# Values of attention A and of the windowed attention, forget gates and shared rotary key made as one block of 680 columns, tokens on partitions, at the start of each layer

## What is computed

```python
h = rms_norm(x, g_mix_pre[i])
z = h @ w_in[i]                                    # 1024 -> 3112 columns
aq, ak, av, af, bcq, bckv, bkpe, cq, ck, cv = jnp.split(z, offsets, axis=-1)
log_f = jax.nn.log_sigmoid(af + b_forget[i])       # 8 forget gates
log_f_cum = jnp.cumsum(log_f, axis=1)
ya = blocked_attention(aq, ak, av, 64 ** -0.5, True, log_f_cum)   # 8 heads of 64
# B: latent attention from bcq, bckv; its rotary key is bkpe (32 columns), shared by the heads
# C: attention over a window of 128, 8 query heads, 2 key/value heads of 64: cq, ck, cv (128 columns)
gates = jax.nn.sigmoid(h @ w_gate[i] + b_gate[i])
merged = ga * (ya @ w_branch_a[i]) + gb * (yb @ w_branch_b[i]) + gc * (yc @ w_branch_c[i])
x = x + rms_norm(merged @ w_out[i], g_mix_post[i])
```

## Time and profile before

| | |
|---|---|
| median of 3 runs | 1970.95 us (1969.31 to 1971.2) |
| the profiled execution | 1971.17 us, span 1969.4 us |
| PE (matmul) busy | 1934.1 us, 98% |
| DVE, ACT, POOL busy | 55%, 42%, 5% |
| DMA | 176.17 MB, 89 GB/s over the span |
| PE's waits on other engines, the longest | `xt` of the residual 8.4, first DMA 4.0, `kB` 2.7, `kC` 2.3 us |

### The profile page before, as it was taken

How to read it: one execution, slowest core, us unless ns; L and a number is a source line. 1 busy time by engine, 2 the same in 40 slices (tenths; PEclk the granted TensorE clock), 3 DMA queues, 4 the chain that set the end, 5 groups by cost and what they waited for, 6 DMA issues and landing times. The chain is left out here.

```text
span 1969.4 us, 25861 instructions
## 1 busy us (share of the span) xinstructions
PE 1934.1 (98%) x9269; PEld 1593.0 (81%) x9269; DVE 1081.1 (55%) x1896; ACT 834.0 (42%) x1417; POOL 107.1 (5%) x85
## 2 busy tenths in 40 slices
PE   8999999999999999999999999999999999999997
PEld 6888887888878888888868888878888788888886
DVE  5444446445477777425674444555445777773266
ACT  4254436543344444314433544455433544442243
POOL 0000000101101111000000000001110011110000
PEclk9999999999999999999999999999999999999999
DMA  5411242213513333332343112421144133333322
GB/s 156 113 40 47 65 97 75 65 43 125 175 32 102 99 95 99 103 111 97 84 124 96 33 54 65 97 76 59 51 150 137 52 98 96 96 97 118 98 84 75
DMA packets 256979, 176.17 MB, mean 89 GB/s; under 512 B 52180, under 2 KB 240880, under 8 KB 256624
## 3 DMA queue, kind: packets, MB, share of 16 engines
q1 hardware_dynamic: 256744, 174.70, 30.2%
q10 hardware_dynamic: 136, 0.16, 0.1%
HBM read 170.44 MB, written 4.36 MB: 89 GB/s over the span
## 5 line engine op out<-in xcount | busy, mean ns | idle before, releaser
L602 PE MATMUL psum<-xnh,wh 128*128 128x512 f32 (+1 forms) x1424 | 573.0, 402 | 7.3 <-DVE kC L1576 2.3
L1307 DVE TENSOR_TENSOR wl<-raw,wh 128x1024 fp32r<-128x1024 f32 (+1 forms) x276 | 363.6, 1317 | 368.9 <-ACT wh L1002 368.2
L602 PE MATMUL psum<-xnh,wl 128*128 128x512 f32 (+1 forms) x1424 | 556.9, 391 | 0.0
L602 PE MATMUL psum<-xnl,wh 128*128 128x512 f32 (+1 forms) x1424 | 556.2, 391 | 0.0
L1002 ACT ACTIVATE wh<-raw 128x1024 fp32r<-128x1024 f32 (+1 forms) x276 | 290.3, 1052 | 422.3 <-PE psum L602 413.1
L602 PEld LDWEIGHTS psum<-xnh,wh 128*128 128x128 f32 (+1 forms) x1424 | 267.3, 188 | 64.9 <-issue 14.9
L602 PEld LDWEIGHTS psum<-xnh,wl 128*128 128x128 f32 (+1 forms) x1424 | 266.6, 187 | 58.9 <-issue 0.5
L602 PEld LDWEIGHTS psum<-xnl,wh 128*128 128x128 f32 (+1 forms) x1424 | 267.3, 188 | 49.9 <-issue 0.2
L1057 ACT ACTIVATE PT<-psum 128x256 f32<-128x256 f32 (+3 forms) x192 | 78.5, 409 | 176.0 <-PE psum L773 175.3
L1450 DVE CUSTOM_DVE_ANT_0 Sp<-psum,ptok 128x128 f32<-128x128 f32 (+3 forms) x128 | 62.5, 489 | 116.2 <-issue 59.5
L602 PE MATMUL psum<-wh,fh 128*128 128x512 f32 x288 | 112.0, 389 | 0.0
(11 more groups left out here) (248 smaller groups left out, 2873.4 us busy)
## 6 DMA issues: line engine op xcount, KB each, us to landing
raw<-in_w_up_dram SPq DMA_DIRECT2D x88, 512.0 KB, 3.7
raw<-in_w_gate_dram SPq DMA_DIRECT2D x48, 512.0 KB, 3.7
raw<-in_w_down_dram SPq DMA_DIRECT2D x44, 512.0 KB, 3.5
raw<-in_w_in_dram SPq DMA_DIRECT2D x40, 512.0 KB, 3.8
raw<-in_w_out_dram SPq DMA_DIRECT2D x16, 512.0 KB, 3.6
raw<-in_w_ple_gate_dram SPq DMA_DIRECT2D x16, 512.0 KB, 3.6
raw<-in_w_in_dram SPq DMA_DIRECT2D x16, 256.0 KB, 3.3
raw<-in_w_branch_a_dram SPq DMA_DIRECT2D x8, 512.0 KB, 3.3
```

What stands on the lines that cost most here:

```text
L602: ins = pe.matmul(out, left, right, start=start and n == 0, stop=stop and n == 2)
L1307: dve.tensor_tensor(low[:, 0:n], raw[(L * NCH + c) % RAW][:, 0:n], hi[:, 0:n].bitcast(F32), ALU.subtract).then_inc(w_lo.sem, 1)
```

## The change

The 512 columns of `vA`, 8 gates, 32 of the shared key and 128 of `vC` are one block of 680 columns, made first in the layer, in eight chunks `first` (one for each 128 input channels, 680 floats wide, three DMAs). Tokens come out on partitions: each chunk is used for 4 blocks of tokens x 2 halves of 340 columns x 3 matmuls, and the eight banks hold all sums. The matmuls of chunks 0 and 1 are done block by block of tokens, since the banks come free in pairs as the norm goes on. ACT evicts the first 340 columns of each block to `vA`, DVE the other 340 in four pieces to `vA`, `kft` (gates and key) and `vC`. `kft` is turned by four transposes beside the first key chunk and copied to `kf`, from where the gates go on as before. The halves of chunks 2 and 3 lie in extra places (`front_x`). `vC` is no longer turned. The stage of attention A begins after the last `qA` chunk and has `qC` x 4, `kC` and the first gate chunk; that of attention C has 11 chunks. The first score steps of attention A wait for the `qA` banks one by one.

```diff
-    [("kf", 0)] + [("kA", m) for m in range(4)] + [("qA", m) for m in range(4)] + [("vA", m) for m in range(4)]
-    + [("qC", m) for m in range(4)] + [("vC", 0), ("kC", 0)]
+    [("first", m) for m in range(KT)] + [("kA", m) for m in range(4)] + [("qA", m) for m in range(4)]
+    + [("qC", m) for m in range(4)] + [("kC", 0)]
...
+ST_KA = KT
+ST_A = ST_KA + 8
...
+EXTRA.update({2: 0, 3: 1})
...
+FW = 340
+WIDTH = {"first": 2 * FW}
+F_GATE, F_PE, F_VC = 512, 520, 552
...
+        if kind == "first":
+            return [(full[:, 0:F_PE], w_in[L, :, m, CA_V:CA_V + 520]),
+                    (full[:, F_PE:F_VC], w_in[L, :, m, CB_PE:CB_PE + 32]),
+                    (full[:, F_VC:2 * FW], w_in[L, :, m, CC_V:CC_V + P])]
...
-                    pe.wait_ge(g_empty.sem, g_empty.at(L, G_BASE[(ST_A, ST_A + 6)[a]]))
+                    pe.wait_ge(g_empty.sem, g_empty.at(L, G_BASE[ST_KA + 4 if a == 0 else ST_A + 5]))
...
+                if a == 0 and i == 0:
+                    pe.wait_ge(g_empty.sem, g_empty.at(L, G_BASE[ST_KA + 4] + h // 2 + 1))
...
+        def first_part(L, m, t):
+            for h in range(2):
+                ins = three(bank[2 * t + h][:, 0:FW], m, FW * h, FW, xnh[:, m, P * t:P * t + P],
+                            xnl[:, m, P * t:P * t + P], m == 0, m == KT - 1, w_moves=True)
+            return ins
+        def first_chunks(L):
+            for m in range(2):
+                pe.wait_ge(w_hi.sem, w_hi.at(L, m + 1))
+                pe.wait_ge(w_lo.sem, w_lo.at(L, m + 1))
+            for t in range(TB):
+                pe.wait_ge(xn_hi.sem, xn_hi.at(L, 2 * t + 2))
+                pe.wait_ge(xn_lo.sem, xn_lo.at(L, 2 * t + 2))
+                for m in range(2):
+                    ins = first_part(L, m, t)
+                    if t == TB - 1:
+                        ins.then_inc(w_used.sem, 1)
+            for m in range(2, KT):
+                pe.wait_ge(w_hi.sem, w_hi.at(L, m + 1))
+                pe.wait_ge(w_lo.sem, w_lo.at(L, m + 1))
+                for t in range(TB):
+                    ins = first_part(L, m, t)
+                    if m == KT - 1 and t < TB - 1:
+                        ins.then_inc(wide_full.sem, 1)
+                ins.then_inc(w_used.sem, 1)
+        def turn_gates(L):
+            b = aux_open(L, "kf")
+            for s in (wide_empty, wide_half):
+                pe.wait_ge(s.sem, s.at(L, TB))
+            for t in range(TB):
+                ins = pe.transpose(b[0:40, P * t:P * t + P], kft[:, t, :], ident)
+            ins.then_inc(aux_full.sem, 1)
+        def beside_first_keys(L, k):
+            if k == 2:
+                for s in (wide_empty, wide_half):
+                    pe.wait_ge(s.sem, s.at(L, 2))
+                spread_scale(L, "0")
+            if k == 6:
+                turn_gates(L)
...
-                if kind == "kC":
-                    pe.wait_ge(g_empty.sem, g_empty.at(L, G_BASE[c]))
-                    o = g_open(1)
-                    for t in range(TB):
-                        ins = pe.transpose(o[:, P * t:P * t + P], th[0][:, P * t:P * t + P], ident)
-                    ins.then_inc(vt_full.sem, 1)
...
-            slot(L, 0)
-            slot(L, 1, beside=lambda k: k == 5 and spread_scale(L, "0"))
-            for c in range(2, ST_A):
+            first_chunks(L)
+            for s in (wide_empty, wide_half):
+                pe.wait_ge(s.sem, s.at(L, 1))
+            slot(L, ST_KA, beside=lambda k: beside_first_keys(L, k))
+            for c in range(ST_KA + 1, ST_A):
...
+            if c < ST_KA and c in EXTRA:
+                act.wait_ge(w_used.sem, w_used.at(L, 0))
+                act.wait_ge(x_summed.sem, x_summed.at(L, TB))
...
+        def first_out(L, t):
+            if t < TB - 1:
+                act.wait_ge(wide_full.sem, wide_full.at(L, t + 1))
+            else:
+                act.wait_ge(w_used.sem, w_used.at(L, ST_KA))
+            act.wait_ge(rcol_ready.sem, rcol_ready.at(L, RB_NORMS.index("0") + 1))
+            act.activation(vA[:, t, 0:FW], bank[2 * t][:, 0:FW], ACT.Copy, scale=rcol[:, t:t + 1]
+                           ).then_inc(wide_half.sem, 1)
...
-            slot(L, 1)
-            slot(L, 2)
+            for c in range(2, ST_KA + 1):
+                hi(L, c)
+            for t in range(TB):
+                first_out(L, t)
+            hi(L, ST_KA + 1)
+            slot(L, ST_KA + 1)
+            slot(L, ST_KA + 2)
...
+        def first_out(L, t):
+            if t < TB - 1:
+                dve.wait_ge(wide_full.sem, wide_full.at(L, t + 1))
+            else:
+                dve.wait_ge(w_used.sem, w_used.at(L, ST_KA))
+            if t == 0:
+                dve.wait_ge(rcol_ready.sem, rcol_ready.at(L, RB_NORMS.index("0") + 1))
+            b, scale = bank[2 * t + 1], rcol[:, t:t + 1]
+            for out, lo_, hi_ in ((vA[:, t, FW:512], FW, F_GATE), (kft[:, t, 32:40], F_GATE, F_PE),
+                                  (kft[:, t, 0:32], F_PE, F_VC), (vC[:, t, :], F_VC, 2 * FW)):
+                ins = dve.tensor_scalar(out, b[:, lo_ - FW:hi_ - FW], scale, None, ALU.mult)
+            ins.then_inc(wide_empty.sem, 1)
...
-            lo(L, 2)
+            for c in range(2, ST_KA):
+                lo(L, c)
+            first_out(L, 0)
+            lo(L, ST_KA)
+            for t in range(1, TB):
+                first_out(L, t)
             scale_rows(L, "0", rb)
-            post(L, 0)
-            for c in range(2, ST_A):
+            lo(L, ST_KA + 1)
+            for c in range(ST_KA + 1, ST_A):
                 slot(L, c)
-                if c == 8:
+                if c == ST_KA + 1:
+                    gates_out(L)
```

More of the change, by code:

```diff
@@ L65, in gate_chunks @@
     return out
-ST_A = 13
+ST_KA = KT
+ST_A = ST_KA + 8
 CHUNKS += gate_chunks(0)
@@ L101, in last_in_slot @@
     return RING[n] if n >= 0 else RING[n] - NCH
-WIDTH = {"kf": KT * 40}
-G_OF = {"vA": 0, "out": 0, "down": 0, "pg": 0, "kC": 2, "uqn": 2, "uqp": 2, "ukn": 4, "ukv": 4, "ple": TB,
+FW = 340
+WIDTH = {"first": 2 * FW}
+F_GATE, F_PE, F_VC = 512, 520, 552
+G_OF = {"first": 0, "out": 0, "down": 0, "pg": 0, "uqn": 2, "uqp": 2, "ukn": 4, "ukv": 4, "ple": TB,
         "branch0": 2, "branch1": 2, "branch2": 2}
@@ L111, in width @@
     return WIDTH.get(CHUNKS[c][0], 1024)
+G_LEFT_OUT = ("out", KT - 1)
 G_BASE = [0]
-for _k, _ in CHUNKS:
-    G_BASE.append(G_BASE[-1] + G_OF.get(_k, 1))
+for _c in CHUNKS:
+    G_BASE.append(G_BASE[-1] + (1 if _c == G_LEFT_OUT else G_OF.get(_c[0], 1)))
 NG = G_BASE[-1]
@@ L342, in trunk_kernel @@
     vC = here("vC", 50, [P, TB, P])
+    kft = here("kft", 112, [P, TB, 40])
     biasC = here("biasC", 52, [P, H, 192])
@@ L387, in trunk_kernel @@
               for e in range(TAIL)]
+    front_x = [(here(f"front_wh{e}", o, [P, 1024], F32R), here(f"front_wl{e}", o + 4, [P, 1024], F32R))
+               for e, o in enumerate((32, 104))]
     def halves(c):
+        if c < ST_KA and c in EXTRA:
+            return front_x[EXTRA[c]]
         if c in EXTRA:
@@ L483, in chunk_dmas @@
         raise ValueError(kind)
-    N_DMA = [{"kf": 2, "qC": 2, "uqn": 4, "uqp": 4, "ukn": 2, "ukv": 2}.get(k, 1) for k, _ in CHUNKS]
+    N_DMA = [{"first": 3, "qC": 2, "uqn": 4, "uqp": 4, "ukn": 2, "ukv": 2}.get(k, 1) for k, _ in CHUNKS]
     LAND = []
@@ L764, in attention @@
                 b = TBK[u % 2]
-                if a == 0 and u == 0:
-                    pe.wait_ge(wide_empty.sem, wide_empty.at(L, TB))
                 if u >= 2:
@@ L813, in g_open @@
                 return G[g % 2]
-            if kind in ("kA", "qA", "qC", "kC", "vC", "zq", "zkv", "up", "kf") or kind[:4] == "gate":
+            if kind in ("kA", "qA", "qC", "kC", "zq", "zkv", "up") or kind[:4] == "gate":
                 o = g_open(0)
-                M = 40 if kind == "kf" else P
                 for k in range(KT):
-                    pre = {"kf": 0, "up": 1}.get(kind)
-                    if pre is not None and m == 0:
-                        pe.wait_ge(xn_hi.sem, xn_hi.at(L, KT * pre + k + 1))
-                        pe.wait_ge(xn_lo.sem, xn_lo.at(L, KT * pre + k + 1))
-                    ins = three(o[0:M, :], c, M * k, M, xnh[:, k, :], xnl[:, k, :], k == 0, k == KT - 1)
+                    if kind == "up" and m == 0:
+                        pe.wait_ge(xn_hi.sem, xn_hi.at(L, KT + k + 1))
+                        pe.wait_ge(xn_lo.sem, xn_lo.at(L, KT + k + 1))
+                    ins = three(o[:, :], c, P * k, P, xnh[:, k, :], xnl[:, k, :], k == 0, k == KT - 1)
                     if k == KT - 1:
@@ L992, in hi @@
                 return
-            if c in EXTRA:
+            if c < ST_KA and c in EXTRA:
+                act.wait_ge(w_used.sem, w_used.at(L, 0))
+                act.wait_ge(x_summed.sem, x_summed.at(L, TB))
+            elif c in EXTRA:
                 act.wait_ge(w_used.sem, w_used.at(L, c - EXTRA[c] - 2))
@@ L1207, in _ @@
             act.activation(PT[0][32:40, :], Pr[1][32:40, :], ACT.Ln, bias=1.0).then_inc(f_log.sem, 1)
```

(11 more changed lines are left out.)

68 lines of the change are left out of this document (22 added, 46 removed).

## The result

The changed kernel takes 1974.63 us (median of 20 runs, 1972.07 to 1976.78), the kernel before in the same session 1971.14 (20 runs, 1969.00 to 1974.34). The ratio is 1.0017, 95% interval [1.0012, 1.0023]: about 3.5 us slower, inside the 3.9 us that I called no change. The forecast was 1972.3.

The account below looks back on a forecast made before the run. PE, busy 98% of the span, was taken as the bound. Layer 1's start +3.95, layer 2's -0.2 and vanished waits -2.4 sum to +1.35 on 1971.17, so 1972.5, less 0.2 for the median: 1972.3 us; range 1966.5 to 1978.

Parts of the forecast that it names:

- Pitch of 340 columns, 0.155: PE's first part: each 340-column matmul starts 0.155 us after the last, 0.1417 for columns plus 0.0133; 192 take 29.8 us.
- The load as the bound: Rival, chance 0.07: weight loads pace the 340-column matmuls at 0.188 us each, costing 12.7 us, for 1985 us.
- Start of layer 1, +3.95: PE idles until 21.02: -0.35 for the earlier key start, +2.6 for more matmuls left, +1.7 for half clock.
- 3.3 us at half speed: Start of layer 1: after PE's idle stretch the clock runs at 1.2 GHz for 3.3 us, costing 1.7.
- Start of layer 2, -0.2: First part of layer 2 takes 33.6 us against 33.8, including a 2.4 us wait for chunk 2's low half.
- The waits that go, -2.4: Both layers: `kf` wait gone, -0.5; `kC` wait gone, -2.3; new waits on attention A's last low half, +0.4.
- the things costed at nothing: First-part eviction, DMA supply, and attention C's 38 steps over 11 chunks instead of 12: priced at no time.
- signs of being wrong: Pitch of 0.15 or below or of 0.19, layer 1 starting before the norm ends, or new attention-stage waits.
- Hand-over at the end of the first part, DMA supply at nothing: DVE's four eviction pieces take about 0.9 us, covered by chunk 7 with 0.4 spare; supply needs 94 GB/s against 96.
- The median: Whole kernel: the median lies 0.2 us below the profiled execution, put at 1972.5, giving 1972.3.
- The second fall of the clock behind the stop in layer 2: Part of a rival, chance 0.13: late key hand-over costs 3.0 us, the clock falling at layer 2's stop 1.7; 1977.
- Cheap columns and no stops: Rival, chance 0.11: pitch 0.1505 (-1.7), clock holds in layer 1 (-1.7), POOL does not delay `row_scales` (-2.4); 1966.5 us.

Follow-up runs that it names:

- run 4: Changed kernel with the 680 columns split as 512 and 168 instead of 340 and 340; median 1978.76 us, ratio 1.0036.
- run 1: Changed kernel with ACT and DVE making the halves of chunk 1 before the norm in layer 1; median 1968.6 us, ratio 0.9989.
- run 3: Changed kernel with 24 useless 512-column matmuls keeping PE at work behind the norm in layer 1; median 1972.12 us, ratio 1.0003.
- run 6: Changed kernel with chunk 1's halves before layer 1's norm, POOL's fill after the row scales, and useless matmuls at the turns; median 1963.13 us.
- run 2: Changed kernel with POOL's fill waiting until DVE has the row scales, in both layers; median 1972.7 us, ratio 1.0004.
- run 9: Changed kernel with DVE filling the corners of attention C's bias early, right behind the last query of C; median 1970.25 us, ratio 0.9989.
- run 12: Changed kernel with only useless matmuls added, at the turn into layer 2 and behind each output projection; median 1974.27 us, ratio 1.0008.
- run 11: Changed kernel with chunk 1's halves early, POOL's fill later, useless matmuls at the turns and the bias's corners early; median 1961.57 us, ratio 0.9941.
- run 10: Changed kernel with `kC` back as last chunk of stage A, one gate chunk ahead of it; median 1976.7 us, ratio 1.0022.
- run 7: Kernel before the change with useless matmuls at the turn into layer 2 and after each output projection; median 1969.68 us, ratio 0.9989.

## Why the prediction was right, and where it was not

That the difference would be below 3.9 us was right, and the sum of the forecast (+1.35) is that of the profiled executions (+1.21). That close a hit is luck: the start of layer 1 came out 0.6 too dear, the waits that go gave 0.55 less than forecast, the last stretch cost 0.3, and a fall of the clock that only the profiled execution of the kernel before had gave 1.57 back. Step by step:

- **Pitch of 340 columns, 0.155.** Right (33 matmuls in the trace). The formula of the Trainium skill (TensorE: Matmul & The Clock Gate, Back-to-back issue gap), which the page gives for the gap by itself and not for a stream of loads and matmuls, gives 0.144 us; neither this nor its 0.216 for 512 columns is what the traces show. By it the 384 matmuls would be 384 x 0.0108 = 4.2 us cheaper, not 4.3.
- **The load as the bound.** It did not come true. Run 4 shows that there is such a bound, at 0.11 and not at the record's 0.19, and that it would have decided had the halves been cut unevenly. The Trainium skill (same page, Part 3, The mechanism) says that a load overlaps a matmul in flight only where their row groups differ, and this is against the trace: load and stream of 340 columns in a row would be 0.25. The same section also lets a load into the background weight buffer run ahead of matmuls, which the 0.155 would fit.
- **Start of layer 1, +3.95.** Measured +4.53. The mechanism is right, and runs 1 and 3 show both parts of it. Mis-sized was the term "3.3 us at half speed": of the 6.8 us of half clock 4.4 fell on matmuls, and 2.0 were lost instead of 1.7. PE also started 0.16 later than at 21.02, and 192 matmuls at full clock take 29.9 (run 6), not 29.8.
- **Start of layer 2, -0.2.** Measured -0.22, with the wait behind POOL's fill that run 2 took away. Inside it the clock was half for longer and the wait shorter by the same amount; the step counted them as if they added, though only the later of the two paths counts.
- **The waits that go, -2.4.** This step failed in part. The waits for `kf` and `kC` went, but the text named `y0l` as what would be late next, at 0.2 a layer, and there was no such wait: nine matmuls stand between, not the six that I counted. Late next were the maxima, behind DVE's fills of the bias, at 1.2 a layer (run 9). "Keys to turn" gained 0.80 and 1.05, not twice 1.2. I had looked for what PE needs first at the border, and not for how far DVE falls behind once PE no longer stops for it. And the stage's 11 chunks instead of 12 stood among the things costed at nothing, "two or three places apart as before": the third and fourth scores moved 0.69 us ahead, more than the 0.48 of the new wait. New waits in the attention stages were on the list of signs of being wrong, and this is one.
- **Hand-over at the end of the first part, DMA supply at nothing.** Right: 0.86 us for the four pieces against 0.9, and the key matmul did not wait.
- **The median.** The step that takes the profiled execution's sum over to the median failed: +3.5 against +1.35. By the mean clock of the runs, the changed kernel sits at 0.993 or 0.994 in 16 of 20, the kernel before at 0.997 in its most frequent group. I had counted the falls of the clock in one execution, as if each always came; they come in some runs and not in others. The four runs at 0.995, the profiled one among them, took 1972.07 to 1973.95, the 16 others 1973.53 to 1976.78, so the clock goes with about 2 us of the gap. It is not all: the six runs at 0.994 are not faster than the ten at 0.993. None of the 16 was profiled, so where their falls lie, and what else they lost, stays open.
- **Rivals.** The second fall of the clock behind the stop in layer 2, priced at 1.7, did not come in the changed kernel and came in run 12, at a stop of 3.03 us. "Cheap columns and no stops" did not come true; edits 1 to 3 are two of its three conditions made by hand.

## What to carry to other kernels

When a merge saves columns, ask first whether the removed work was the filler of a stretch where its engine had nothing else to do: here the `kf` matmuls were free in layer 1, and what took their place had to wait for a chunk that was made too late. Then follow the engine that the removed waits had given time to; the next wait shows in its queue, not in that of the engine that waits. Where work is spread over a number of chunks and that number changes, work out its places again: here one k-step was enough to matter. And a wait is worth more than its listed idle time if short dependent instructions stand behind it, and less if another late path ends just after it: take both away together, or neither pays.

## What the runs showed of the hardware

- The same small DVE operation (128x4) takes 0.16 us alone and 3.46 beside POOL's fill of one partition x 4096, ending with the fill; two subtractions of 128x680 keep their 0.82 each, the second wholly beside the same fill (run 2). Which operations are held up, and by what, was not tried further.
- Around PE's idle time at the start of layer 1 the clock stood at half for 3.4 us (runs 1, 11), 6.8 (the changed kernel, runs 2, 4, 9) or 10.2 (runs 10, 12). How long the idle time was does not settle it: in the profile of run 11 it fell with 2.19 us idle, in that of run 6 it stood through 2.77.
- Runs of the kernel before sort by mean clock, 0.998 down to 0.994, over most of their spread of 5.5 us. With useless matmuls at the turns eleven runs lie within 0.9 us, all at 0.997 or 0.998 (run 7).
- Behind one another matmuls of 168 columns go at 0.11 us (0.070 for the columns), the pace of the weight loads in a row; those of 340 go at 0.155, which is their columns, 0.142, and 0.013 on top (run 4, the changed kernel).
